# A feed-forward down-projection turned round: weights stationary instead of activations, with norm and layout change moved to match

## The reference

```
h = rms_norm(x, norm_mlp_pre)           # 512 x 1024
f = relu(h @ w_ff1) ** 2                # 512 x 4096
y = f @ w_ff2                           # 512 x 1024
out = x + rms_norm(y, norm_mlp_post)    # mean over the 1024 features of a token
```

## Time and profile before

| what | us |
|---|---|
| median of three runs (3603.61 to 3606.54) | 3603.97 |
| the execution that was profiled | 3606.54 |
| its span, first to last instruction | 3604.7 |
| PE busy, share of the span | 3382.1 (94%) |
| DVE busy | 1238.0 (34%) |
| ACT busy | 1027.9 (29%) |
| POOL busy | 197.6 (5%) |
| mean granted TensorE clock, share of full speed | 0.977 |

### The profile page before, as it was taken

One profiled execution on the slowest core, in us unless ns is written; L12 is line 12 of the kernel. 1 busy time (PEld: TensorE's weight loads), 2 busy tenths in 40 slices (PEclk: granted clock), 3 DMA queues, 4 the chain that ended last, 5 costly groups with the idle time before them and its releaser, 6 DMA issues.

```text
span 3604.7 us, 48687 instructions
## 1 busy us (share of the span) xinstructions
PE 3382.1 (94%) x21618; PEld 2272.1 (63%) x21618; DVE 1238.0 (34%) x1742; ACT 1027.9 (29%) x1644; POOL 197.6 (5%) x118
## 2 busy tenths in 40 slices
PE   7999999999899999989999998998879999989998
PEld 5787667887544443467768874333227766858886
DVE  3235642323411111144663433111124434353333
ACT  3523541213210000046453232000022344343323
POOL 0100000211100000001000211000001010020000
PEclk9999999999899999999999999999999999989999
DMA  7440014222499889822103328999982121323331
GB/s 227 133 137 24 1 57 120 59 65 98 171 375 396 349 338 399 325 57 82 36 1 82 94 76 314 409 403 409 409 312 76 37 62 30 94 59 94 98 99 65
DMA packets 360129, 601.35 MB, mean 167 GB/s; under 512 B 48786, under 2 KB 242672, under 8 KB 359792
## 3 DMA queue, kind: packets, MB, share of 16 engines
q1 hardware_dynamic: 357024, 596.62, 46.6%
q10 hardware_dynamic: 2896, 1.61, 0.2%
HBM read 596.09 MB, written 2.10 MB: 166 GB/s over the span
## 4 chain that ended last, share of the span: by engine, by line
PE 85%; DMA 6%; DVE 5%; ACT 2%; issue 1%; ACTq 0%; POOL 0%; DVEq 0%; SPq 0%
PE ps L581 32%; PE ps L1925 6%; PE ps L2292 5%; PE ps L1075 4%; PE ps L1920 4%; PE ps L633 3%; PE ps L1164 3%; PE ps L1928 3%; PE ps L1959 3%; PE ps L1125 3%; PE ps L1339 3%; DMA ring<-in_w_e_down 3%; DMA ring<-in_w_e_up 3%; PE ps L602 2%; PE ps L1955 2%; PE ps L1572 2%
## 5 line engine op out<-in xcount | busy, mean ns | idle before, releaser
L581 PE MATMUL ps<-xh,wh 128*128 128x512 f32 x1912 | 647.2, 376 | 22.4 <-DVE xl L2142 12.2
L581 PE MATMUL ps<-xh,wl 128*128 128x512 f32 x1912 | 630.8, 368 | 0.0
L581 PE MATMUL ps<-xl,wh 128*128 128x512 f32 x1912 | 629.8, 367 | 0.0
L554 DVE TENSOR_TENSOR wl<-ring,wh 128x1024 fp32r<-128x1024 f32 (+1 forms) x259 | 333.9, 1289 | 444.4 <-ACT wh L545 442.8
L581 PEld LDWEIGHTS ps<-xh,wh 128*128 128x128 f32 x1912 | 330.2, 189 | 109.0 <-issue 36.1
L545 ACT ACTIVATE wh<-ring 128x1024 fp32r<-128x1024 f32 (+1 forms) x259 | 272.1, 1051 | 423.8 <-PE ps L581 163.2
L581 PEld LDWEIGHTS ps<-xl,wh 128*128 128x128 f32 x1912 | 329.8, 189 | 63.3 <-issue 4.5
L581 PEld LDWEIGHTS ps<-xh,wl 128*128 128x128 f32 x1912 | 329.4, 189 | 61.5
L1925 PE MATMUL ps<-ring,arena 128*32 128x512 f32 x2048 | 267.2, 593 | 1.0 <-DVE arena L1707 1.0
L1920 PE MATMUL ps<-ring,arena 128*64 128x512 f32 x984 | 228.4, 601 | 18.1 <-DMA ring<-in_w_e_up 9.0
L1920 PEld LDWEIGHTS ps<-ring,arena 128*64 128x64 f32 x984 | 66.6, 137 | 157.3 <-issue 103.5
(11 more groups left out here) (277 smaller groups left out, 4332.7 us busy)
## 6 DMA issues: line engine op xcount, KB each, us to landing
ring<-in_w_e_gate SPq DMA_DIRECT2D x128, 1024.0 KB, 9.2
ring<-in_w_e_down SPq DMA_DIRECT2D x128, 1024.0 KB, 8.1
ring<-in_w_e_up SPq DMA_DIRECT2D x123, 1024.0 KB, 9.0
ring<-in_w_in SPq DMA_DIRECT2D x116, 512.0 KB, 3.9
ring<-in_w_ada SPq DMA_DIRECT2D x96, 512.0 KB, 4.8
ring<-in_w_ff SPq DMA_DIRECT2D x64, 512.0 KB, 3.9
ring<-in_w_out SPq DMA_DIRECT2D x24, 512.0 KB, 3.7
ring<-in_w_in SPq DMA_DIRECT2D x40, 256.0 KB, 3.9
```

The costliest lines, as they stand in the source:

```text
L554: e.tensor_tensor(m.WL[:, o:o + many], halves.aps[s][:, 0:many], m.WH[:, o:o + many].bitcast(F32), ALU.subtract).then_inc(*lo.up(X.key, q))
L581: i = e.matmul(ps[0:M, a:b], w[:, k, 0:M], h[:, k, a:b], start=k == 0 and p == 0, stop=k == 7 and p == 2)
```

## The change

The second product is turned round. Now the weights are stationary: for each of the 8 feature groups d, 128 x 128 of `w_ff2` are loaded and the 512 tokens of `FF` stream past, so that y comes out with features on partitions, one PSUM half-tile (`accs(d)`) per d. A unit is 8 d x 3 passes = 24 matmuls of 512 columns. For f = 0 and 1, whose activations lie in two pieces of 256 tokens, it is 48 of 256 columns. All four PSUM tiles are taken ahead of the first matmul. The norm is made over partitions with the helpers named above: two of the eight tiles are first copied to `Y_`, since the sum of squares needs their PSUM tile. The sum goes into `XT`, and the transposes stand at the end: 4 groups of 8, drained by ACT and DVE in turn and sent out in natural token order. The transposes behind f1 units 4 to 7, their drains, the gain's DMA and the row norm are gone.

```diff
@@ pe_second
             for f in range(32):
                 pe_linear3(e, X2, ("f1", f), ...)
-                if 4 <= f < 8:
-                    ps, when = bank.take(("back", f - 4), c_out.at("fin", "back", f - 4))
-                    ...
-                    for k in range(KD):
-                        i = e.transpose(ps[:, k * 128:(k + 1) * 128], X_(k)[:, f - 4], ident)
+            held = []
+            for n, freed in enumerate(((c_out.at("fin", 6), d_out.at("fin", 7)), (d_out.at("fin", "y", 1),),
+                                       (d_out.at("fin", "y", 3),), (d_out.at("fin", "y", 5),))):
+                ps, when = bank.take(("acc", n), *freed)
+                held.append(ps)
+                for w in when:
+                    e.wait_ge(*w)
             for f in range(32):
                 ...
-                for c in range(4):
-                    for p, (h, w) in enumerate(((x2.XH, wh), (x2.XH, wl), (x2.XL, wh))):
-                        for n in (0, 512):
-                            i = e.matmul(ps[:, n:n + 512], ff_part(h, f)[c], w[:, 0, n:n + 512], ...)
-                    if f == 31 and c < 3:
-                        i.then_inc(*p_out.up("acc", c))
+                for d in range(KD):
+                    for p, (w, h) in enumerate(((wh, x2.XH), (wh, x2.XL), (wl, x2.XH))):
+                        for n in (0, 1) if f < 2 else ():
+                            i = e.matmul(accs(d)[:, 256 * n:256 * n + 256], w[:, 0, d * 128:(d + 1) * 128], ff_part(h, f)[:, n], ...)
+                        if f > 1:
+                            i = e.matmul(accs(d), w[:, 0, d * 128:(d + 1) * 128], ff_part(h, f), ...)
                 i.then_inc(*dn.up("x2", X2.unit["f2", f]))
+            pe_norm_take(e, "ne")
+            for k in range(KD):
+                pe_square(e, "ne", k, KD, NX, sqr[k % 2])
+            for c in range(4):
+                ps, when = bank.take(("out", c), ...)
+                for k in range(KD):
+                    e.wait_ge(*(l_an if k % 2 else d_out).at("fin", "x", k))
+                    i = e.transpose(ps[:, k * 128:(k + 1) * 128], XT[:, k, c * 128:(c + 1) * 128], ident)
+                i.then_inc(*p_out.up("out", c))
@@ act_second
-            e.dma_start(gain, I["norm_mlp_post_2"]...broadcast_to([128, D])).then_inc(s_sk, 16)
...
-                if 4 <= f < 8:
-                    e.activation(BACK[f - 4], quarters(bank.of["back", f - 4]), ACT.Copy)...
...
-            e.activation(sm[:, 16:17], eps[:, 0:1], ACT.Ln, ...)
-            for c in range(4):
-                e.activation(SQ[c], quarters(bank.of["acc", c]), ACT.Square, accum_out=ssq[:, c:c + 1])...
-            e.activation(scale, ssq, ACT.Ln, bias=eps[:, 0:1], scale=1.0 / D)...
-            e.activation(scale, scale, ACT.Exp, scale=-0.5)...
-            e.activation(OUT[0], OUT[0], ACT.Copy, scale=scale[:, 0:1])...
+            e.activation(Y_[:, 0, :], accs(6), ACT.Copy).then_inc(*c_out.up("fin", 6))
+            for k in range(KD):
+                ...
+                act_square(e, "ne", k, Y_[:, k - 6, :] if k > 5 else accs(k), NX, sqr)
+            act_rstd(e, "ne", KD, NX, D)
+            for c in (0, 2):
+                e.activation(OUT[:, c, :], bank.of["out", c][:, :], ACT.Copy)...
@@ dve_second
-            for c in range(4):
-                e.tensor_tensor(OUT[c], quarters(bank.of["acc", c]), quarters(gain), ALU.mult)...
-            for c in range(1, 4):
-                e.scalar_tensor_tensor(out=OUT[c], in0=OUT[c], scalar=scale[:, c:c + 1], in1=BACK[c], op0=ALU.mult,
-                                       op1=ALU.add)...
+            e.tensor_copy(Y_[:, 1, :], accs(7)).then_inc(*d_out.up("fin", 7))
+            dve_add_normed(e, d_out, ("ne", "fin"), lambda k: Y_[:, k - 6, :] if k > 5 else accs(k), 40)
+            for c in (1, 3):
+                e.tensor_copy(OUT[:, c, :], bank.of["out", c][:, :])...
@@ pool_second
-            e.tensor_tensor(OUT[0], OUT[0], BACK[0], ALU.add)...
+            pool_add_normed(e, d_out, "fin")
@@ sp_program
-            ov = out[0].rearrange("(i r) (a n) -> i r a n", r=4, a=4)
-            for c in (1, 2, 3, 0):
+            ov = out[0].rearrange("(c p) d -> p c d", p=128)
+            for c in range(4):
```

More of the change, by code:

```diff
@@ L2125, in build @@
         QC, KV, KP, OB = ch(12288, 4), ch(14336, 2), ch(15360, 1), ch(15360, 4)
[L2126 to L2130, removed]
+        MX, FO, FF, Y_ = ch(2048, 8), ch(6144, 8), ch(0, 32), ch(16384, 2)
+        OUT = AR(Z + 4096, 4096).rearrange("p (c d) -> p c d", c=4)
         X2 = WX[2]
@@ L2283, in pe_second @@
                 e.wait_ge(*lo.at("x2", X2.units[X2.unit["f2", f]][1] - 1))
[L2284 to L2292 removed]
+                for d in range(KD):
+                    for p, (w, h) in enumerate(((wh, x2.XH), (wh, x2.XL), (wl, x2.XH))):
+                        for n in (0, 1) if f < 2 else ():
+                            i = e.matmul(accs(d)[:, 256 * n:256 * n + 256], w[:, 0, d * 128:(d + 1) * 128], ff_part(h, f)[:, n],
+                                         start=f == 0 and p == 0 and n == 0, stop=False, skip_group_check=True)
+                        if f > 1:
+                            i = e.matmul(accs(d), w[:, 0, d * 128:(d + 1) * 128], ff_part(h, f), start=False, stop=f == 31 and p == 2,
                                          skip_group_check=True)
[L2294 to L2295 removed]
                 i.then_inc(*dn.up("x2", X2.unit["f2", f]))
+            pe_norm_take(e, "ne")
+            for k in range(KD):
+                pe_square(e, "ne", k, KD, NX, sqr[k % 2])
+            for c in range(4):
+                ps, when = bank.take(("out", c), d_out.at("fin", "out", c) if c % 2 else c_out.at("fin", "out", c))
+                for w in when:
+                    e.wait_ge(*w)
+                for k in range(KD):
+                    e.wait_ge(*(l_an if k % 2 else d_out).at("fin", "x", k))
+                    i = e.transpose(ps[:, k * 128:(k + 1) * 128], XT[:, k, c * 128:(c + 1) * 128], ident)
+                i.then_inc(*p_out.up("out", c))
         def ff_part(t, f):
[L2300 to L2302 removed]
             return aside(t, f) if f < 2 else t[:, f % 8, 0:NX]
@@ L2306, in halved, with accs @@
             return t.rearrange("p (h t) -> p h t", h=2) if f < 2 else t
-        def multiplied_out(c):
-            return p_out.at("acc", c) if c < 3 else dn.at("x2", X2.unit["f2", 31])
+        def accs(d):
+            return bank.of["acc", (d // 2 + 1) % 4][:, 512 * (d % 2):512 * (d % 2) + 512]
         sqm = [tmp[:, 4096:4608], tmp[:, 4608:5120]]
@@ L2421, in act_second @@
                     ahead(f + 3)
-            e.activation(sm[:, 16:17], eps[:, 0:1], ACT.Ln, bias=eps[:, 0:1]).then_inc(*n_ln.up("set"))
-            for c in range(4):
[L2424 to L2432, removed]
+            e.wait_ge(*dn.at("x2", X2.unit["f2", 31]))
+            e.activation(Y_[:, 0, :], accs(6), ACT.Copy).then_inc(*c_out.up("fin", 6))
+            for k in range(KD):
+                if k == 6:
+                    e.wait_ge(*c_out.at("fin", 6))
+                if k == 7:
+                    e.wait_ge(*d_out.at("fin", 7))
+                act_square(e, "ne", k, Y_[:, k - 6, :] if k > 5 else accs(k), NX, sqr)
+            act_rstd(e, "ne", KD, NX, D)
+            for c in (0, 2):
+                e.wait_ge(*p_out.at("out", c))
+                e.activation(OUT[:, c, :], bank.of["out", c][:, :], ACT.Copy).then_inc(*c_out.up("fin", "out", c))
         def dve_norm(e, stage, dst, kn, base):
@@ L2532, in dve_second @@
                     ahead(f + 3)
-            e.wait_ge(s_sk, 32)
-            for c in range(4):
[L2535 to L2538, removed]
-            for c in range(1, 4):
-                e.wait_ge(*d_out.at("fin", "y", c))
-                e.scalar_tensor_tensor(out=OUT[c], in0=OUT[c], scalar=scale[:, c:c + 1], in1=BACK[c], op0=ALU.mult,
-                                       op1=ALU.add).then_inc(*d_out.up("fin", "out", c))
+            e.wait_ge(*dn.at("x2", X2.unit["f2", 31]))
+            e.tensor_copy(Y_[:, 1, :], accs(7)).then_inc(*d_out.up("fin", 7))
+            dve_add_normed(e, d_out, ("ne", "fin"), lambda k: Y_[:, k - 6, :] if k > 5 else accs(k), 40)
+            for c in (1, 3):
+                e.wait_ge(*p_out.at("out", c))
+                e.tensor_copy(OUT[:, c, :], bank.of["out", c][:, :]).then_inc(*d_out.up("fin", "out", c))
         def pool_second(e):
```

18 lines of the change are left out of this document (4 added, 14 removed).

## The result

The changed kernel takes 3623.49 us in the median of four runs (3622.10 to 3625.45), the kernel before 3605.26 us beside it (3603.61 to 3607.30, four runs). The ratio is 1.0052, with a 95% interval of 1.004 to 1.0064: about 18 us slower. The forecast was 3622.7 us and +18.7 us.

The account below looks back on a forecast made before the run. PE, busy for 94% of the span, was taken to bound the kernel up to f2's end, with a tail behind it. Tail +21.3 us and PE's stream -2.6 us gave +18.7 on 3603.97: 3622.7 us, range 3618 to 3629.

Parts of the forecast that it names:

- Which stretch decides: Whole kernel: an edit costs only what it adds to PE's stream up to f2's end or to the tail behind it.
- The product itself: f2 on PE: 24 matmuls of 512 columns per unit cost 0.227 us each in both forms, so 30 units stay equal.
- The rival on the other side: f2 on PE: weights stationary shorten each matmul, 0.193 in place of 0.227 us, giving 3596.8 us; chance 0.02.
- The wait and the small matmuls: Start of f2: PE waits 0.82 us for ACT's last f1 drain; 256-column matmuls in units 0 and 1 add 0.62 us.
- Squares and factor: Tail's first steps: eighth square ends about 7.45 us behind f2, then two table loads, Ln and Exp take 3.93 us.
- The sum into the residual: Tail, DVE and POOL behind the factor: 14.78 us, as in the stage "no"; 13.9 us by the Trainium skill's rule.
- The transposes: Tail, PE: 25 in a row behind the last addition, 7 then 11 per us, 3.7 us; clock at 0.50 before them.
- Drain and output: Tail's end: DVE's copy out of PSUM takes 1.23 us, then the output 4.1 us.
- Short tail: Tail and f2's start: all doubtful terms fall at their low ends, +14.5 us, 3618.5 us; chance 0.10.
- Half clock in the sums: Tail's sums of squares on PE: the clock falls when f2 ends, up to +6.5 us, 3629 us; chance 0.10.
- The change doesn't put the steps on the path: Tail: sum and transposes overlap f2's end; with half the tail hidden, +8 us, 3612 us; chance 0.04.

## Why the prediction was right

**Which stretch decides.** Right. PE has no gap behind f1 in either kernel but the new one of 0.98 us, and the edit was worth what it did to PE's stream (-2.15 us, forecast -2.60) and to the tail (+21.30, forecast +21.3).

**The product itself.** Right: weights or activations stationary, 0.227 us per matmul. The rival on the other side had this as its point, and it falls.

**The wait and the small matmuls.** The mechanism was right and shown by taking the wait away. I set 0.82 + 0.62; it was 0.98 + 0.87. The drain ended 0.63 us after f1 and not 0.80, PE went on 0.35 us after that and not 0.02, and the restart took 0.24 us; without a gap the small matmuls cost 11.51 - 2 x 5.44 = 0.63 us, as forecast.

**Squares and factor.** Right to 0.13 us, from a norm of four tiles in another place. Its squares read SBUF; of the eight here two do, and six read PSUM.

**The sum into the residual.** Right in kind, 0.94 us too dear. I took the row of the stage "no" whole, though its operands lie in SBUF, and had 13.9 us only as a remark.

**The transposes.** The step that was sized worst: 3.7 for 5.66 us. The clock was at 0.50, as said. But 7 and 11 were counts and not rates, which is 0.8 us of the miss (4.5 and not 3.7), and the full rate came later than in the burst I read, which is the other 1.2.

**Drain and output.** 1.1 us too dear: here each of the four output DMAs landed after 2.6 us. The median of 3.2 that I took was of outputs that followed each other closer; with the transposes made faster it was 3.2 here too.

**The rivals.** "Short tail" had two of its four parts, the additions (two of three at 1.53) and the landing (2.6 us), for -0.94 and -1.12 us; the transposes and the wait went the other way. Its -1.0 for the landing was not worked out: 2.7 in place of 3.2 us gives -0.5. "Half clock in the sums" is refuted by the granted clock of 1.00. "The change doesn't put the steps on the path" is refuted by leaving the norm out: its 7.53 + 3.98 = 11.51 us went, 0.69 of them came back as a copy, and the faster transposes gave 1.03 more, which leaves 11.85 expected against 11.57 measured.

## What to carry to other kernels

Behind the last matmul every step has its full price, so before turning a last product round for its own sake, write down what its result's layout asks of the norm, the residual and the store: here equal matmuls, but 21 us of steps behind them. A sum over chunks of a row can be finished chunk by chunk: let the pieces of the last product end one by one, and let each be finished by itself. With a lighter factor and without POOL beside DVE this was worth 6 us here, of which 2.7 came from groups that end further apart. When a small figure is to be forecast from another stage's row, check in which memory its operands lie and what clock it ran at, and take a rate from a length and a number of instructions, never from the counts of neighbouring stretches.

## What the runs showed that I had not expected

- The same 25 transposes of 128x128 took 5.61, 5.34, 4.87 and 4.63 us in four kernels with the same code there, as the granted clock came back at different points of the burst, or not at all within it.
- ACT's operations out of PSUM overlap: 512 columns start 0.48 us apart and are listed with 0.60, 1024 columns with their row sum follow after 1.00 us and not after 1.23. A sum of listed durations is too high for a row of them.
- Making transposes faster by 2.44 us brought 1.4 us of tail, as the outputs then landed after up to 3.7 us in place of 2.6.
